# One expert pair with 128 places for its second expert, in place of a separate pass over an over-full expert

## The reference, cut to what matters

```python
logits = jnp.dot(h, w_router) + b_router            # 320 tokens x 32 experts
top_logit, top_e = lax.top_k(logits, 4)
gate = jax.nn.softmax(top_logit, axis=-1)
def expert_block(xb, e):                            # rows of one expert
    gu = xb @ w_gu[e] + b_gu[e]                     # 1024 -> 2048
    glu = jnp.minimum(gu[:, 0::2], 7.0)
    lin = jnp.clip(gu[:, 1::2], -7.0, 7.0)
    act = glu * jax.nn.sigmoid(1.702 * glu) * (lin + 1)
    return act @ w_down[e] + b_down[e]              # 1024 -> 1024
# out[token] += gate * expert_block(token's row, its expert), for each of its 4 experts
```

## Time and profile before

| | us |
|---|---|
| median of 3 runs | 1506.03 (1503.15 to 1506.78) |
| the profiled execution's own time | 1503.66 |
| its span, first to last instruction | 1501.9 |
| TensorE busy | 1412.1 (94%) |
| VectorE, ScalarE, GpSimd busy | 586.4, 381.4, 207.1 |
| mean granted TensorE clock | 0.985 of full |
| HBM read over the span | 483.13 MB |

### The profile page before, as it was taken

One profiled execution on the slowest core, in us unless ns is written; L12 is line 12 of the kernel. 1 busy time (PEld: TensorE's weight loads), 2 busy tenths in 40 slices (PEclk: granted clock), 3 DMA queues, 4 the chain that ended last, 5 costly groups with the idle time before them and its releaser, 6 DMA issues.

```text
span 1501.9 us, 22013 instructions
## 1 busy us (share of the span) xinstructions
PE 1412.1 (94%) x8520; PEld 825.1 (55%) x8521; DVE 586.4 (39%) x1280; ACT 381.4 (25%) x643; POOL 207.1 (14%) x304
## 2 busy tenths in 40 slices
PE   7999999999999999989989999989999889999996
PEld 6988888889998443433434434433443433434432
DVE  6778897876543252222113112212231222113214
ACT  6557777665321320100001001000100100001002
POOL 4034544536800000000000000000000000000000
PEclk9999999999999999999999999999999999999998
DMA  8435555554454789999999999998999999999996
GB/s 268 145 92 150 158 175 162 168 168 140 154 158 163 323 356 396 425 429 428 429 429 428 429 428 429 429 429 361 425 426 431 428 427 430 428 429 430 426 425 242
DMA packets 125742, 495.33 MB, mean 330 GB/s; under 512 B 7293, under 2 KB 95421, under 8 KB 100025
## 3 DMA queue, kind: packets, MB, share of 16 engines
q1 hardware_dynamic: 87616, 471.75, 77.7%
q10 hardware_dynamic: 35904, 18.88, 4.3%
q0 software_dynamic: 2160, 3.87, 0.8%
HBM read 483.13 MB, written 11.34 MB: 329 GB/s over the span
## 4 chain that ended last, share of the span: by engine, by line
PE 65%; DMA 28%; DVE 3%; SPq 1%; ACT 1%; issue 1%; POOL 1%; DVEq 0%; ACTq 0%; POOLq 0%
DMA ring_b<-in_w_gu 25%; PE bank L1430 18%; PE bank L1526 8%; PE bank L1252 7%; PE bank L922 5%; PE bank L931 4%; PE bank L903 3%; PE bank L1367 3%; PE bank L927 2%; PE bank L924 2%; PE bank L1268 2%; DMA ring<-in_w_gu 1%; PE bank L1161 1%; PE bank L1581 1%; DMA ring<-in_w_down 1%
## 5 line engine op out<-in xcount | busy, mean ns | idle before, releaser
L1430 PE MATMUL bank<-ring_b,xe 128*64 128x512 f32 x1248 | 342.7, 612 | 36.7 <-DMA ring_b<-in_w_gu 36.7
L1430 PEld LDWEIGHTS bank<-ring_b,xe 128*64 128x64 f32 x1248 | 113.2, 140 | 250.3 <-issue 249.6
L1430 PE MATMUL bank<-ring,xe 128*64 128x512 f32 x768 | 226.0, 594 | 4.8 <-DMA ring<-in_w_gu 4.6
L1526 PE MATMUL bank<-ring,actT 128*64 128x512 f32 x720 | 213.0, 596 | 0.0
L1645 ACT ACTIVATE swi<-swi 128x256 f32<-128x256 f32 x66 | 27.3, 416 | 551.6 <-DVE swi L2604 520.8
L2604 DVE TENSOR_SCALAR swi<-bank 128x256 f32<-128x256 f32 x60 | 25.5, 425 | 313.1 <-PE bank L1430 308.3
L1252 PE MATMUL bank<-rounded,ring_r 128*128 128x320 f32 x912 | 133.8, 308 | 1.7 <-DVE ring_r L2431 1.7
L1252 PEld LDWEIGHTS bank<-rounded,ring_r 128*128 128x128 f32 x912 | 132.8, 188 | 2.8 <-DVE ring_r L2431 2.4
L875 POOL TENSOR_TENSOR kept<-take 128x256 bf16<-128x256 bf16 x15 | 9.2, 613 | 848.5 <-PE bank L1508 848.5
L1430 PEld LDWEIGHTS bank<-ring,xe 128*64 128x64 f32 x768 | 74.6, 137 | 76.3 <-issue 76.3
L1526 PE MATMUL bank<-ring_b,actT 128*64 128x512 f32 x240 | 105.8, 593 | 4.3 <-ACT actT L2028 4.3
(11 more groups left out here) (373 smaller groups left out, 1985.3 us busy)
## 6 DMA issues: line engine op xcount, KB each, us to landing
ring_b<-in_w_gu SPq DMA_DIRECT2D x79, 2048.0 KB, 17.0
ring<-in_w_gu SPq DMA_DIRECT2D x49, 2048.0 KB, 16.7
ring<-in_w_down SPq DMA_DIRECT2D x47, 2048.0 KB, 18.7
ring<-in_w_in SPq DMA_DIRECT2D x32, 1024.0 KB, 5.5
ring_b<-in_w_down SPq DMA_DIRECT2D x15, 2048.0 KB, 14.4
arena<-in_state_ssm ACTq DMA_DIRECT2D x16, 512.0 KB, 5.0
out<-arena ACTq DMA_DIRECT2D x16, 512.0 KB, 3.7
ring<-in_w_branch_ssd SPq DMA_DIRECT2D x8, 1024.0 KB, 5.4
```

What stands on the lines that cost most here:

```text
L1430: mm = pe.matmul(bank[q][side(h), :], xe[:, j, side(h)], moe_slot(2 * i + h, first)[:, 2 * FF * k + 512 * q:2 * FF * k + 512 * q + 512], s ...
L1526: mm = pe.matmul(bank[4 + half][side(h), :], actT[:, f, side(h)], w[:, D * k + 512 * half:D * k + 512 * half + 512], start=False, stop=(f ...
```

## The change

One pair, DOUBLE = 7, has room for 128 rows of its second expert (position SWAP = 15). The first over-full expert with a number from 4 to 31, found at run time, changes places with expert 15: VectorE's new `exchange` rewrites the tables (`row_expert`, `slot_no`, `gates3`, the new `expert_at`) at the end of pair 0, and SyncE reads the experts to load from `expert_at`, two register loads a pair. Levels beyond it are still listed for extra passes, now after pair 8 (HALF = 9); with one expert over 64 and under 129 rows, `more` becomes 0 and the pass is skipped.

The work of the extra rows moves into the pairs: their gather (72 matmuls) into pair 6 after j = 3; their gate/up and down steps into pair 7 behind each chunk's own steps, so that the second expert's chunk serves both; their combination into pair 8's `combine`, six float32 matmuls between those of `ye_hi` and `ye_lo`. Loads of pair 2 and later wait for `exchange`.

```diff
-HALF = NP // 2
+DOUBLE = NP // 2 - 1
+HALF = DOUBLE + 2
+SWAP = 2 * DOUBLE + 1
...
+            load_pair(1, (2, 3))
             sp.wait_ge(S["work_ready"], 1)
+            with sp.Fori(2, HALF) as n:
+                load_pair(n, experts_of(n))
...
-            def combine(n):
+            def combine(n, double=False):
...
+                    if double:
+                        pe.matmul(bank[6 + i % 2][:, :], takeT_extra[side(half), P * c:P * c + P],
+                                  ye_extra[side(half), :], start=False, stop=False)
...
-                    pe.wait_ge(S["work_ready"], 1)
+                    pe.wait_ge(S["place_ready"], 3)
...
+                    if double and q == 3:
+                        double_step(pe, "act", "out")
...
+                    if j == 3 and inputs:
+                        double_step(pe, "dve", "select")
+                        pe.wait_ge(S["cm_done"], n * 6)
+                        gather(take_extra).then_inc(S["extra_pe"], 1)
...
+            def gate_up_double(n):
...
+                def more_slots(j):
...
+                    for b in range(2):
+                        for h in range(2):
+                            at = 2 * FF * k + 512 * (2 * h + b)
+                            mm = pe.matmul(bank[4 + b][side(h), :], xe_extra[:, j, side(h)],
+                                           moe_slot(2 * i + 1)[:, at:at + 512], start=False, stop=(j == KD - 1))
...
+                for i in range(GU_CHUNKS):
+                    both(2 * i)
+                    both(2 * i + 1)
+                    if i == 0:
+                        combine(n - 1)
+                        double_step(pe, "dve", "bias")
+                        for b in range(2):
...
+                    more_slots(2 * i)
+                    more_slots(2 * i + 1)
+
+            def down_double(n):
+
+                double_step(pe, "dve", "lin1")
+                for half in range(2):
+                    pe.matmul(bank[4 + half][:, :], pick_bias[:, :], bd_parts[:, hb(0, half)],
+                              start=True, stop=False)
...
+                for f in range(DOWN_ROWS):
+                    both(f)
...
+                turn_kept(take_extra, 512)
+                turn_kept(kept).then_inc(S["tk_psum"], 1)
+                gates_of_kept(take_extra, SWAP, 1, 6)
+                gates_of_kept(kept, n * 2, 2).then_inc(S["kept_used"], 1)
+                double_step(pe, "dve", "act1")
...
+                both(DOWN_ROWS)
+                double_step(pe, "act", "acts_turned")
+                for f in range(DOWN_ROWS):
+                    more_slots(f)
+                for f in range(DOWN_ROWS + 1, KD):
+                    both(f)
+                for f in range(DOWN_ROWS, KD):
+                    more_slots(f)
...
+                    if f == 5 and first:
                         pe.wait_ge(S["place_ready"], 1)
+                        pe.matmul(bank[2][:, 1:2], before[:, :], over, start=True, stop=True)
+                        pe.matmul(bank[2][:, 3:4], ones[:, :], star, start=True, stop=True)
+                        pe.matmul(bank[2][0:1, 2:3], over, ones[:, 0:1], start=True, stop=True
+                                  ).then_inc(S["place_psum"], 1)
...
-            with pe.Fori(1, HALF) as n:
+            with pe.Fori(1, DOUBLE - 1) as n:
                 block_of(n)
...
+            block_of(DOUBLE - 1, inputs=True)
+            gate_up_double(DOUBLE)
+            dispatch(DOUBLE + 1)
+            turn_act(DOUBLE)
+            down_double(DOUBLE)
+            pe.wait_ge(S["work_ready"], 1)
             more = pe.value_load(work[0:1, 40:41], min_val=0, max_val=MAX_EXTRA)
+            block_of(DOUBLE + 1, double=True)
...
+            def exchange():
+
+                dve.wait_ge(S["place_ready"], 3)
+                link(dve.tensor_scalar(star, delta, float(SWAP), None, ALU.add))
+                link(dve.tensor_scalar(back, delta, -1.0, None, ALU.mult))
+                link(dve.tensor_copy(work[0:1, 61:62], star[0:1]))
+                exchanged(row_expert[:, :], row_expert[:, :], take_first[0:96, 0, :], take_first[0:96, 1, :], 96)
+                exchanged(expert_at[0:1, :], slots[0:1, 0:E], take_first[0:1, 0, 0:E], take_first[0:1, 1, 0:E], 1)
+                e = dve.value_load(work[0:1, 61:62], min_val=4, max_val=E - 1)
```

More of the change, by code:

```diff
@@ L302, in build @@
         over = part(1)
+        eligible = part(1)
+        cand = part(1)
+        first_over = part(1)
+        star = part(1)
+        delta = part(1)
+        back = part(1)
+        swap_slots = part(3, 1)
+        swap_gates = part(3, 3)
+        listed = part(MAX_EXTRA)
+        moved_list = part(MAX_EXTRA)
         places = part(MAX_EXTRA)
@@ L1405, in combine_last, with gate_up @@
                               start=False, stop=True).then_inc(S["cm_psum"], 1)
-            def gate_up(n, more16, first=False, before_it=False, last=False, extras=None):
+            def gate_up(n, more16, first=False, before_it=False, last=False, extras=None, double=False, inputs=False):
                 if first:
@@ L2557, in _ @@
             dve.wait_ge(S["cnt_psum"], 1)
-            dve.tensor_tensor(over, bank[4][:, 0:1], levels, ALU.is_gt).then_inc(S["cnt_ready"], 1)
+            link(dve.tensor_tensor(over, bank[4][:, 0:1], levels, ALU.is_gt))
+            dve.tensor_tensor(cand, over, eligible, ALU.mult).then_inc(S["cnt_ready"], 1)
             def take_free(n):
@@ new lines, in list_extras @@
+                link(dve.tensor_tensor(over, over, first_over, ALU.subtract))
+                dve.scalar_tensor_tensor(star, numbers, -float(SWAP), first_over, ALU.add, ALU.mult
+                                         ).then_inc(S["place_ready"], 1)
+                dve.wait_ge(S["place_psum"], 2)
+                dve.tensor_scalar(places, slots[:, 0:MAX_EXTRA], bank[2][:, 1:2], over, ALU.is_equal, ALU.mult
+                                  ).then_inc(S["place_ready"], 1)
+                link(dve.tensor_copy(work[0:1, 40:41], bank[2][0:1, 2:3]))
@@ new lines, in list_extras, with exchanged @@
+                link(dve.tensor_copy(delta, bank[2][:, 3:4]))
+                dve.wait_ge(S["place_psum"], 3)
+                dve.tensor_copy(work[0:1, 41:41 + MAX_EXTRA], bank[3][0:1, 0:MAX_EXTRA]
+                                ).then_inc(S["place_ready"], 1)
+            def exchanged(out, of, a, b, r):
+                link(dve.tensor_scalar(a, of, star[0:r], back[0:r], ALU.is_equal, ALU.mult))
+                link(dve.tensor_scalar(b, of, float(SWAP), delta[0:r], ALU.is_equal, ALU.mult))
+                link(dve.tensor_tensor(a, a, b, ALU.add))
+                link(dve.tensor_tensor(out, of, a, ALU.add))
@@ new lines, in block_double @@
+            def block_double(n, used):
+                add_up(n - 1)
+                take_free(n + 1)
+                select_pair(n * 2 + 2)
+                swiglu(n, used - 1)
+                read_inputs(n + 1)
+                dve.wait_ge(S["at_psum"], 2 * n + 2)
+                for b in range(2):
+                    v = bank[4 + b][:, :].rearrange("p (f two) -> p f two", two=2)
+                    if b == 0:
+                        double_step(dve, "pe", "gate_up0")
+                    else:
+                        dve.wait_ge(chunk_used, used)
+                    dve.tensor_scalar(glu[:, b, :], v[:, :, 0], LIMIT, None, ALU.min).then_inc(S["extra_dve"], 1)
+                    dve.tensor_scalar(lin[:, b, :], v[:, :, 1], -LIMIT, LIMIT, ALU.max, ALU.min
+                                      ).then_inc(S["extra_dve"], 1)
+                for b in range(2):
+                    double_step(dve, "dve", f"lin{b}")
+                    dve.scalar_tensor_tensor(lin[:, b, :], lin[:, b, :], 1.0, glu[:, b, :], ALU.add, ALU.mult
+                                             ).then_inc(S["extra_dve"], 1)
+                for b in range(2):
+                    double_step(dve, "dve", f"prod{b}")
+                    double_step(dve, "act", f"sig{b}")
+                    dve.tensor_tensor(lin[:, b, :], lin[:, b, :], sig[:, b, :], ALU.mult).then_inc(S["extra_dve"], 1)
+                double_step(dve, "dve", "act1")
+                slot_gates(n, True)
+                pick_pair(n * 2 + 2)
+                split_out(n)
```

221 lines of the change are left out of this document (175 added, 46 removed).

## The result

The changed kernel takes 1490.12 us (median of 4 runs, 1487.89 to 1490.59), the kernel before 1505.31 (1503.15 to 1506.78). The ratio is 0.9899, 95% interval 0.9888 to 0.9911: 15.2 us faster. The profiled execution took 1490.59, its span is 1488.2. The forecast was 1490.0. The next sections show which terms carried it and which errors nearly cancelled.

A forecast was written before the change was run, and what follows sets the result against it. DMA bound the kernel, by 4.8 us a pair over TensorE. 35.5 us removed less 18.4 new idling (17.2 by two roads), less 1.2 early, gives 16.0 off: 1490.0 on the median; ends 1484.5 and 1497, 76% within 1485 to 1494.

The forecast's parts named there:

- What is taken away, 35.5 us: The extra pass between pairs 7 and 8: 29.3 us for six chunk loads plus 6.2 of dry DMA behind it.
- Pair 6, 0: The extra gather, 4.23 us, costs 0 in pair 6: the existing wait and half clock cover it.
- Pair 7, 78.5: Pair 7 on TensorE takes 53.85 plus 24.6 us of extra work, 78.5, waiting for no weights; ends 77 and 81.
- rival E: Granted clock falls to half in pair 7; for all its added 24.6 us the time is 1514; 3%.
- Pair 8, 58.2: Pair 8 takes 53.85 plus 4.4 us for its longer combine, 58.2; ends 57.5 and 61.
- rival C: Each of twelve tile-form changes in pair 8's combine drains the array: 4.7 us in place of 0.5, 1494; 6%.
- DMA idle 18.4 against 6.2: Late chunk releases in pairs 7 and 8 idle DMA for 18.4 us; the dry stretch behind the old pass was 6.2.
- the second road: Saving counted by pair starts: pair 9 starts at 1066.3, not 1083.6, so 17.3 us.
- Pairs 0 and 1, 1.2: Longer list work and `exchange` make TensorE 1.2 us late in pair 1, all counted; ends 0 and 5.
- Rival B: `exchange` ends near 600, TensorE stands 9 to 10 us in pair 1's combine: 1498 to 1499; 10%.
- A (the ring takes up the lag): Queued loads cover TensorE's lag, DMA stays busy, all of 35.5 us is won: 1472; 3%.
- D: The slot isn't taken, the pass stays, and pairs 7 and 8 carry the extra work: 1525 or more; 2%.

The follow-up runs named there:

- e8: Kernel before, no extra pass (expert 5's rows 65 to 75 left out), count loaded ahead of pair 7, TensorE's output waits only inside the branch: 1468.86 us, one run.
- e6: Kernel before with the list's thresholds raised, so no extra pass runs (expert 5's rows 65 to 75 left out): 1475.72 us, one run.
- e11: Changed kernel with TensorE's three waits and register load put back between pairs 8 and 9 for every number of passes: 1490.44 us.
- e3: Changed kernel without two of the three bf16 parts of the extra rows' gather in pair 6 (48 of 72 matmuls): 1491.35 us, one run.
- a_again: The changed kernel unedited, measured once more: 1490.83 us.
- e5: Changed kernel with e1's edit and `exchange` moved behind VectorE's adds of pair 0's combination: 1485.23 us.
- e1: Changed kernel, pair 8's combine with two more banks and both extra matmuls of a row block side by side: 1484.90 us.
- e4: Changed kernel without 12 of the 16 extra down matmuls in pair 7: 1485.14 us, one run.

## Why the prediction was right, point by point

- **What is taken away, 35.5 us.** The sum fits what pass and barrier cost together (36, e8). Its parts were put down too simply: taking the pass alone away gave 29.1 (e6), since the wait between pairs 7 and 8, which I hadn't priced, then left DMA dry for as long as the pass had. So the 6.2 of dry DMA aren't the pass's alone; how they divide in the kernel before isn't shown. In the changed kernel they are gone either way: with the barrier put back between pairs 8 and 9 the time is the same (e11). Whether it would cost between pairs 7 and 8 there wasn't run.
- **Pair 6, 0.** Right: 58.2 us for 58.6 before, and e3 the same time.
- **Pair 7, 78.5.** 77.7 in the profile, 77.7 to 80.3 over all kernels whose wide pair is as in the change. Extra gate/up 13.7 for 14.0, down 6.9 for 7.0, turns 0.7 for 0.8; the second kept set 0.6 and the stall 1.3 as forecast. That the clock could fall behind this stall was not in the sum (rival E had it at far more); it does in three of these profiles (`a_again`, e3, e5), at 1.5 to 1.7 us. And "no weights are waited for" fails by 0.5 us in `a_again`.
- **Pair 8, 58.2.** This term was mis-sized: 60.3. I took 0.5 for twelve changes of tile form; they cost 0.38 a step, 2.3 in all. I had read "no gap" off one change, from full-width bias matmuls to column tiles, and carried it over to half-height ones. The Trainium skill ("TensorEngine Tiling (Array Packing)", Key Properties) says that a change of tiling mode drains TensorE; the trace agrees here, at half of what rival C had at its dearest, though it did not in my row, which was of another kind.
- **DMA idle 18.4 against 6.2.** 19.0 against 6.4 (860 to 1100 us; 21.8 in `a_again`, where the clock fell). The pieces of my 18.4 add to 18.0; the second road, 17.3, is the one that the runs bear out: a microsecond of TensorE in pairs 7 and 8 is about one of the kernel (e1, e4).
- **Pairs 0 and 1, 1.2.** TensorE was late by more (0.9 at the start of pair 1, then 1.2 in combine: 2.1), DMA lost less by it: 0.6 to 0.8. `exchange` took 7.5 us for 6 and ended at 593.8, 591.6 without the 2.2 us by which that profile's pair 0 was late, forecast 591. Rival B needed 600.
- **The sum.** Pair 8 was 2.1 dearer, pair 7 0.8 cheaper, the early loss 0.4 to 0.6 less, and the first weight load started 1.1 later in the profile of after. The medians differ by 15.2 for 16.0 forecast. Part of the exact hit is luck: the forecast stood on the median of three earlier runs, 0.7 above the later one. The upper end of the range, 1497, is less than its own pieces give (1490.0 + 2.5 + 2.8 + 3.8 = 1499); the result lies far from it.
- **Rivals.** A (the ring takes up the lag) and E (half clock throughout) are out, D too: one pass less was read.

## What to carry to other kernels

Where transfers set the time, write the time as bytes plus idle DMA, and price an edit by the idling it adds; a compute engine's slack per stage and the loads in flight absorb little once a stage exceeds both. Work that is moved into a stage is free only as far as it fills a wait that the stage has anyhow. Before pricing a block that is taken out, look at the waits around it that stand outside its branch: they may leave the same idle stretch when the block doesn't run. And where a kernel jumps over a block, look for packets of the instruction queues before calling the gap behind it the price of the jump.

## What had not been expected

- Two float32 matmuls over 64 rows each and 512 columns, in different halves of the array's rows, took 1.06 us together (e1), with 0.18 of that, by subtraction, for the change of form; alone between full-height ones each took 1.05 (the changed kernel).
- A stall of 2 us in two pieces left the granted clock at 1.0 in some executions and brought it to 0.5 in others of the same kernel (7.02 and 8.62 us for the same 32 records).
- A jump over a block that isn't run cost nothing in eight profiles and 2.2 us in a ninth with the same code there (e3), in which an instruction packet came late.
- A late TensorE costs by where it is late: 9.8 us between pairs 7 and 8 of the kernel without a pass cost about 7 (e6 against e8), 4.1 us between pairs 8 and 9 of the changed kernel nothing that shows (e11).
